# The first microseconds of a decoder layer: x and the first weight unit loaded in quarters by turns, the transposes of x spread around the first products

## The reference

```
x = x + 0.5 * swiglu(rms_norm(x, norm_ffn1), ffn1_gate, ffn1_up, ffn1_down)
h = rms_norm(x, norm_mix)
proj = h @ w_in                          # MoBA q k v | RWKV r k v | gate_A gate_B
y_a = moba_attention(qa, ka, va, rel_bias)
y_b = rwkv7_time_mix(h, rb, kb, vb, ...)
x = x + (sigmoid(ga) * (y_a @ proj_a) + sigmoid(gb) * (y_b @ proj_b)) @ w_out
x = x + 0.5 * swiglu(rms_norm(x, norm_ffn2), ffn2_gate, ffn2_up, ffn2_down)
return rms_norm(x, norm_final)
```

## Time and profile before

| what | us |
|---|---|
| median of 3 runs | 637.8 (637.66 to 638.42) |
| the profiled execution's own time | 637.18 |
| span of its trace, first to last instruction | 635.4 |
| TensorE busy | 626.1 (99% of the span) |
| VectorE busy | 422.8 (67%) |
| ScalarE busy | 295.6 (47%) |
| GpSimd busy | 91.3 (14%) |
| read from memory | 103.48 MB |

### The profile page before, as it was taken

One profiled execution on the slowest core, in us unless ns is written; L12 is line 12 of the kernel. 1 busy time (PEld: TensorE's weight loads), 2 busy tenths in 40 slices (PEclk: granted clock), 3 DMA queues, 4 the chain that ended last, 5 costly groups with the idle time before them and its releaser, 6 DMA issues.

```text
span 635.4 us, 15491 instructions
## 1 busy us (share of the span) xinstructions
PE 626.1 (99%) x6736; PEld 611.8 (96%) x6736; DVE 422.8 (67%) x491; ACT 295.6 (47%) x343; POOL 91.3 (14%) x91
## 2 busy tenths in 40 slices
PE   9999999999999999999999999999999999999996
PEld 9999999999999999999988999999999999999996
DVE  5856887665556369958994437977766666665662
ACT  6643555443334264525655545645544444443341
POOL 0017700000114000020004533006000000000120
PEclk9999999999999999999999999999999999999998
DMA  9686666545555246693242232346555566546541
GB/s 310 202 257 198 182 195 198 189 158 201 168 184 184 81 134 199 199 195 124 83 134 69 70 102 79 130 165 195 177 173 185 192 198 197 184 157 206 173 141 66
DMA packets 100640, 105.38 MB, mean 166 GB/s; under 512 B 2228, under 2 KB 98716, under 8 KB 100596
## 3 DMA queue, kind: packets, MB, share of 16 engines
q1 hardware_dynamic: 99380, 101.46, 49.5%
q0 software_dynamic: 1056, 3.02, 2.2%
q10 hardware_dynamic: 160, 0.27, 0.1%
HBM read 103.48 MB, written 1.25 MB: 165 GB/s over the span
## 4 chain that ended last, share of the span: by engine, by line
PE 90%; DVE 5%; DMA 2%; ACT 2%; issue 0%; DVEq 0%; ACTq 0%
PE two L1448 26%; PE two L1449 24%; PE two L1450 24%; PE two L1444 12%; DMA w_raw<-in_ffn_up 2%; DVE w_lo L894 2%; DVE hlo_f L913 1%; ACT w_hi L526 1%; DVE w_lo L904 1%; PE two L1716 1%; PE two L1717 1%; PE two L1718 1%; PE two L1859 0%; ACT KK L782 0%; PE two L1646 0%
## 5 line engine op out<-in xcount | busy, mean ns | idle before, releaser
L526 ACT ACTIVATE w_hi<-w_raw 128x2048 fp32r<-128x2048 f32 (+1 forms) x87 | 164.2, 1888 | 254.9 <-PE two L1450 220.1
L894 DVE TENSOR_TENSOR w_lo<-w_raw,w_hi 128x2048 fp32r<-128x2048 f32 (+1 forms) x87 | 202.4, 2326 | 85.9 <-ACT w_hi L526 85.5
L1448 PE MATMUL two<-hlo_f,w_hi 128*128 128x256 f32 x640 | 178.7, 279 | 1.0 <-DVE w_lo L894 0.9
L1449 PE MATMUL two<-hhi_f,w_lo 128*128 128x256 f32 x640 | 179.2, 280 | 0.0
L1450 PE MATMUL two<-hhi_f,w_hi 128*128 128x256 f32 x640 | 178.9, 280 | 0.0
L1448 PEld LDWEIGHTS two<-hlo_f,w_hi 128*128 128x128 f32 x640 | 120.3, 188 | 2.4 <-DVE w_lo L894 2.4
L1450 PEld LDWEIGHTS two<-hhi_f,w_hi 128*128 128x128 f32 x640 | 120.3, 188 | 0.0
L1449 PEld LDWEIGHTS two<-hhi_f,w_lo 128*128 128x128 f32 x640 | 120.2, 188 | 0.0
L1448 PE MATMUL two<-hid_lo_t,w_hi 128*128 128x256 f32 x352 | 98.6, 280 | 0.0
L1449 PE MATMUL two<-hid_hi_t,w_lo 128*128 128x256 f32 x352 | 98.4, 280 | 0.0
L1450 PE MATMUL two<-hid_hi_t,w_hi 128*128 128x256 f32 x352 | 98.3, 279 | 0.0
(11 more groups left out here) (339 smaller groups left out, 987.3 us busy)
## 6 DMA issues: line engine op xcount, KB each, us to landing
w_raw<-in_ffn_up SPq DMA_DIRECT2D x21, 1024.0 KB, 5.3
w_raw<-in_ffn_gate SPq DMA_DIRECT2D x20, 1024.0 KB, 5.4
w_raw<-in_w_in SPq DMA_DIRECT2D x20, 1024.0 KB, 5.0
w_raw<-in_ffn_down SPq DMA_DIRECT2D x16, 896.0 KB, 4.6
w_raw<-in_ffn_down SPq DMA_DIRECT2D x8, 1024.0 KB, 4.9
w_raw<-in_w_out SPq DMA_DIRECT2D x4, 1024.0 KB, 4.9
w_raw<-in_proj_a SPq DMA_DIRECT2D x4, 512.0 KB, 3.4
w_raw<-in_proj_b SPq DMA_DIRECT2D x4, 512.0 KB, 4.2
```

What stands on the lines that cost most here:

```text
L526: nc.scalar.activation(whi[slot][:, 0:kts], raw[slot][:, 0:kts], ACT.Copy).then_inc(sg["hi_ready"], 1)
L894: nc.vector.tensor_tensor(wlo[slot][:, 0:kts], raw[slot][:, 0:kts], whi[slot][:, 0:kts].bitcast(F32), ALU.subtract).then_inc(sg["lo_ready" ...
L1448: mm(dst, whi[slot][:, k_, cols], xl, start=start, stop=False)
L1449: mm(dst, wlo[slot][:, k_, cols], xh, start=False, stop=False)
```

## The change

- x is loaded in four quarters of 256 features (`x_in0` to `x_in3`), in turn with the four quarters of unit 0. The first four of these eight transfers are issued at once; each later one waits for the landing of an earlier one. The halves of unit 1 and `raw2` then wait for `x_in2`, `x_in3` and `w0_in3`.
- TensorE warms six times instead of seven, transposes the gain row, then the first two quarters of x, warms twice, transposes the third quarter, warms once, and begins unit 0. The fourth quarter of x is transposed behind the first 12 products of unit 0 (`if n + pair == 0`).
- Semaphores are joined: the gain row counts on `first_in` (then 32), `x_T` counts the gain row's transpose first (so `h_hi` waits for j + 2), and ScalarE takes the vectors behind `bias_row`, which is set by the product of `rel` that follows the vectors' transpose.
- ScalarE rounds each quarter of unit 0 behind a semaphore of its own; the squares of x wait for two quarters.

```diff
--- before.py
+++ after.py
@@ -119,7 +119,7 @@
 
 
 SIGNALS = """
-x_in0 x_in1 w0_mid w0_in w1_in vec_in first_in const_in gain1_in gain1_T gain1_ready vecT x_T x_loaded vec_ready
+x_in0 x_in1 x_in2 x_in3 w0_in1 w0_in2 w0_in3 w1_in vec_in first_in const_in gain1_ready x_T x_loaded vec_ready
 hi_ready lo_ready multiplied
 first_hi first_lo first_norm sq_one sq_sum last_sq mean_sq rms_ready rstd_ready gained hhi_ready hlo_ready
 gate_taken up_taken silu_done hid_prod hid_hi hid_lo down_first x_ffn_even x_ffn_odd
@@ -335,21 +335,30 @@
 
             xs = A["x"][0].rearrange("(j p) d -> p j d", p=P)
             sp.dma_start(cst[:, 0:C_FIRST], consts[:, 0:C_FIRST]).then_inc(sg["first_in"], 16)
-            for half in range(2):
-                ds = slice(half * D // 2, (half + 1) * D // 2)
-                sp.dma_start(x_tok[:, :, ds], xs[:, :, ds]).then_inc(sg[f"x_in{half}"], 16)
+
+            def x_quarter(q):
+                ds = slice(q * D // 4, (q + 1) * D // 4)
+                sp.dma_start(x_tok[:, :, ds], xs[:, :, ds]).then_inc(sg[f"x_in{q}"], 16)
 
             for f, base, down in FFN:
                 if f == 0:
+                    x_quarter(0)
                     sp.dma_start(raw[0][:, 0:2], gate_w[0][:, 0:2, 0:W]).then_inc(w_landed[0], 16)
-                    sp.dma_start(raw[0][:, 2:4], gate_w[0][:, 2:4, 0:W]).then_inc(sg["w0_mid"], 16)
+                    x_quarter(1)
+                    sp.dma_start(raw[0][:, 2:4], gate_w[0][:, 2:4, 0:W]).then_inc(sg["w0_in1"], 16)
                     sp.wait_ge(sg["x_in0"], 16)
-                    sp.dma_start(raw[0][:, 4:KD], gate_w[0][:, 4:KD, 0:W]).then_inc(sg["w0_in"], 16)
+                    x_quarter(2)
+                    sp.wait_ge(w_landed[0], 16)
+                    sp.dma_start(raw[0][:, 4:6], gate_w[0][:, 4:6, 0:W]).then_inc(sg["w0_in2"], 16)
                     sp.wait_ge(sg["x_in1"], 16)
+                    x_quarter(3)
+                    sp.wait_ge(sg["w0_in1"], 16)
+                    sp.dma_start(raw[0][:, 6:KD], gate_w[0][:, 6:KD, 0:W]).then_inc(sg["w0_in3"], 16)
+                    sp.wait_ge(sg["x_in2"], 16)
                     sp.dma_start(raw[1][:, 0:4], up_w[0][:, 0:4, 0:W]).then_inc(sg["w1_in"], 16)
-
-                    sp.wait_ge(w_landed[0], 16)
+                    sp.wait_ge(sg["x_in3"], 16)
                     sp.dma_start(raw[1][:, 4:KD], up_w[0][:, 4:KD, 0:W]).then_inc(w_landed[1], 16)
+                    sp.wait_ge(sg["w0_in3"], 16)
                     sp.dma_start(raw2, gate_w[0][:, :, W:2 * W]).then_inc(w_landed[0], 16)
                     sp.dma_start(cst[:, C_FIRST:C_ALL], consts[:, C_FIRST:C_ALL]).then_inc(sg["const_in"], 16)
                     for name in list(VECS)[1:]:
@@ -530,8 +539,8 @@
 
             def first_hi(n, i):
 
-                if n == 0 and i < 3:
-                    act.wait_ge((w_landed[0], sg["w0_mid"], sg["w0_in"])[i], 16)
+                if n == 0:
+                    act.wait_ge((w_landed[0], sg["w0_in1"], sg["w0_in2"], sg["w0_in3"])[i], 16)
                 elif n == 1 and i % 2 == 0:
                     act.wait_ge(w_landed[1] if i else sg["w1_in"], 16)
                 ks_ = slice(2 * i, 2 * i + 2)
@@ -547,7 +556,7 @@
             def h_hi(q, j, dst):
 
                 if q == 0:
-                    act.wait_ge(sg["x_T"], j + 1)
+                    act.wait_ge(sg["x_T"], j + 2)
                 elif q == 1:
                     act.wait_ge(sg["x_ffn_even"], j + 2)
                     act.wait_ge(sg["x_ffn_odd"], j + 2)
@@ -594,7 +603,7 @@
 
                 body(0, nexts(0) if f else [lambda: None, nexts(0)[1]])
                 if f == 0:
-                    act.wait_ge(sg["vecT"], 1)
+                    act.wait_ge(sg["bias_row"], 1)
                     nc.scalar.activation(vec[:, KD:NVEC], bank[5][:, KD:NVEC], ACT.Copy).then_inc(sg["vec_ready"], 1)
                 if f == 0:
                     for i in range(1, 8):
@@ -616,7 +625,7 @@
                     if s % 3 == 2 and s < NDOWN - 1 and f == 0:
                         h_hi(1, s // 3, hhi_m)
 
-            vector_rows(act, "norm_ffn1", sg["gain1_in"])
+            vector_rows(act, "norm_ffn1", sg["first_in"])
             act.wait_ge(sg["x_ffn_odd"], 1)
             nc.scalar.activation(idle[:, 0:1], idle[:, 0:1], ACT.Sqrt)
             act.wait_ge(sg["gain1_ready"], 1)
@@ -624,7 +633,8 @@
                 h_hi(0, j, hhi_f)
                 first_hi(0, j)
             for j in range(4):
-                act.wait_ge(sg[f"x_in{j // 2}"], 16)
+                for q in (0, 1) if j < 2 else (2, 3):
+                    act.wait_ge(sg[f"x_in{q}"], 16)
                 nc.scalar.activation(h_f[:, 2 * j:2 * j + 2].rearrange("p m t -> p (m t)"),
                                      x_tok[:, j % 2, j // 2 * (D // 2):(j // 2 + 1) * (D // 2)], ACT.Square,
                                      accum_out=tok[:, j:j + 1]).then_inc(sg["first_norm"], 1)
@@ -1031,7 +1041,7 @@
             nc.vector.memset(silu[:, 0, 0:P], 1.0).then_inc(sg["x_ffn_even"], 1)
             nc.vector.memset(idle[:], 0.0).then_inc(sg["x_ffn_odd"], 1)
 
-            dve.wait_ge(sg["gain1_T"], 1)
+            dve.wait_ge(sg["x_T"], 1)
             nc.vector.tensor_copy(vec[:, 0:KD], bank[5][:, 0:KD]).then_inc(sg["gain1_ready"], 1)
             dve.wait_ge(sg["gain1_ready"], 1)
             for j in range(4):
@@ -1505,6 +1515,8 @@
                             part(dst, whi[s][:, c, cols], hlo_f[:, c], m + c == 0)
                             part(dst, wlo[s][:, c, cols], hhi_f[:, c])
                             last = part(dst, whi[s][:, c, cols], hhi_f[:, c])
+                    if n + pair == 0:
+                        x_transposed(3)
                 last.then_inc(sg["multiplied"], 1)
 
             def ffn(f, base, down, q):
@@ -1522,7 +1534,7 @@
                     first_chunk(2)
                     pe.wait_ge(sg["vec_in"], 16 * len(VECS))
                     pe.wait_ge(sg["gain1_ready"], 1)
-                    nc.tensor.transpose(bank[5][:, 0:NVEC], vec_rows[:], ident[0:NVEC, 0:NVEC]).then_inc(sg["vecT"], 1)
+                    nc.tensor.transpose(bank[5][:, 0:NVEC], vec_rows[:], ident[0:NVEC, 0:NVEC])
                     pe.wait_ge(sg["const_in"], 16)
                     pe.wait_ge(sg["x_loaded"], 4)
                     mm(bank[6][0:H, 0:384], rel[:], cst[0:NB, C_HOT:C_HOT + 384], start=True, stop=True)\
@@ -1563,19 +1575,23 @@
                     part(bank[4][:, 0:P], silu[:, 0, 0:P], silu[:, 0, 0:P], True)
 
             pe.wait_ge(sg["x_ffn_even"], 1)
-            warm(7)
-            pe.wait_ge(sg["first_in"], 16)
-            pe.wait_ge(sg["gain1_in"], 16)
-            nc.tensor.transpose(bank[5][:, 0:KD], vec_rows[0:KD], ident[0:KD, 0:KD]).then_inc(sg["gain1_T"], 1)
-            warm(1)
-            for q in range(4):
-                pe.wait_ge(sg[f"x_in{q // 2}"], 16)
+            warm(6)
+            pe.wait_ge(sg["first_in"], 32)
+            nc.tensor.transpose(bank[5][:, 0:KD], vec_rows[0:KD], ident[0:KD, 0:KD]).then_inc(sg["x_T"], 1)
+
+            def x_transposed(q):
+                pe.wait_ge(sg[f"x_in{q}"], 16)
                 for c in range(2):
                     for j in range(2):
                         last = nc.tensor.transpose(bank[X_BANKS[q]][:, c * T + j * P:c * T + (j + 1) * P],
                                                    x_tok[:, j, (2 * q + c) * P:(2 * q + c + 1) * P], ident)
                 last.then_inc(sg["x_T"], 1)
-            warm(5)
+
+            x_transposed(0)
+            x_transposed(1)
+            warm(2)
+            x_transposed(2)
+            warm(1)
             ffn(0, N_FFN1, N_DOWN1, 0)
```

## The result

The changed kernel takes 639.32 us (median of 20 runs, 637.3 to 641.73), the kernel before 637.81 (20 runs, 635.75 to 641.9). The ratio is 1.0027, 95% interval 1.0018 to 1.0037: slower by 1.7 us, with 1.2 and 2.4 as ends. Forecast were no measurable change and 637.6, with 639.2 as the upper end.

The account below looks back on a forecast made before the run. TensorE, busy 99%, was taken as the bound, with early loads and splits setting its product at 39.31. Profiled 637.18 less 0.25 gave 636.93, on the median 637.55, said as 637.6; 8 in 10 from 636.7 to 639.2.

Parts of the forecast that it names:

- The landings: First transfers of x and unit 0: x0 lands at 4.21, each later quarter 0.78 us after, w3 at 9.7.
- The load of unit 3: Weight load on the chain, issued at 17.71 before: foreseen 0.25 us earlier, at 17.46, with its 5.52 us unchanged.
- the sum: Whole kernel: 637.18 less 0.25 for the shifted load gives 636.93; on the median 637.55, said as 637.6.
- Rival 2: First transfers: the queue runs thin with two or three quarters in flight, +0.1 to +0.4 us, 638.0; chance 0.20.
- the table: Foreseen landings at the start: x0 4.21, w0 4.99, x1 5.77, w1 6.55, x2 7.33, w2 8.1, x3 8.9, w3 9.7.
- Rival 1: Start of TensorE: first products reached at half pace, +1.3 us (+0.5 to +2.4), 639.1; chance 0.20.
- The front: First transposes and rounding: x0's transposes at 4.25, ScalarE's `hhi` at 5.41 instead of 6.31, 0.9 us early.
- pair 1 eats the gain: Unit 0 on TensorE: x3's transposes take 0.44 us before pair 1, leaving 0.4 of the 0.8 gained.
- SyncE's own queue: Issuing of transfers: SyncE free at about 16.7, 0.8 us of cover before the load of unit 3 at 17.46.
- The rest at nothing: Other parts of the change, such as SyncE's later issues and the vectors' later transpose: hidden, costing nothing.
- The range: Whole kernel's time: 636.7 to 639.2 us for 8 in 10; 637.1 to 638.0 for the forecast alone.

Follow-up runs that it names:

- g_half: Kernel before with the first quarter of unit 0 issued between the two halves of x; ratio 1.0034 (1.0018 to 1.0050).
- after: First trace of the changed kernel itself; 638.06 us in the profiled execution, 639.32 us as median of its runs.
- after2: The changed kernel once more, unaltered, for a second trace of its start; 637.65 us in that trace.
- a_nowait: Changed kernel without SyncE's waits between the first ten transfers, raw2 issued behind w0's landing; ratio to the kernel before 1.0033 (1.0018 to 1.0048).
- b_loads: Changed kernel's loads and waits alone, with TensorE's order of the kernel before; ratio to the kernel before 1.0055 (1.0034 to 1.0076).
- f_deep: Changed kernel without the three waits ahead of unit 1's halves and raw2; ratio to the kernel before 1.0012 (1.0001 to 1.0022).
- h_warm: Changed kernel with three warms ahead of x1's transposes and four behind, instead of none and two; ratio to the kernel before 1.0028 (1.0015 to 1.0042).
- k_deepwarm: Changed kernel without the waits ahead of unit 1's halves and raw2, plus more warms in TensorE's holes; ratio to the kernel before 1.0014 (1.0001 to 1.0027).
- i_x4r2: Kernel before with x in four transfers of 256 KB in 2 KB rows, timed and traced a second time; ratio 1.0011 (0.9999 to 1.0024).
- m_gdeep: Kernel before with a quarter of unit 0 between x's halves and no SyncE wait for x's second half ahead of unit 1; ratio 1.0053 (1.0040 to 1.0066).
- g_half2: Kernel before with a quarter of unit 0 between the halves of x, once more for a second trace; 638.79 us in that trace.
- c_pe: Changed kernel's TensorE order alone, with the loads and waits of the kernel before; ratio to the kernel before 1.0010 (0.9995 to 1.0025).

## Why the prediction was wrong

- **The landings** failed, and with them the forecast. "The size of a transfer thus does not matter while others are queued, and a quarter costs 0.78" was taken from halves and quarters that came one kind after the other. By turns it does not hold: x2 landed at 8.1 and 8.2 against 7.33, x3 at 10.2 and 10.5 against 8.9, w3 at 11.5 and 11.2 against 9.7. The loads alone cost 0.55%, one quarter of weights between two halves 0.34%, both with what the late x then does to TensorE.
- **The load of unit 3** was the other term: the sum let it move "if both loads take as long as before". In the first trace it was issued at 18.65, 1.2 behind the 17.46 of the forecast, and took 6.98 for the 5.52 of the earlier trace rows; so of the 2.4 that unit 3 is late, 0.9 lie before the issue and 1.5 in the load. In the second trace it was issued at 19.90 and took 5.54.
- **Rival 2** was the right mechanism for the part behind 8 us, and its sign (SyncE's waits over 0.3 later than the table) was there in both traces. It was given +0.1 to +0.4. Taking the three later waits away gave back more than half of the 1.7 (1.0027 to 1.0012) and again half (1.0028 to 1.0014), about 0.9 us each time. What was missed in it is that a late queue also lengthens the load that the chain crosses, and that "`raw2` is needed by ScalarE only after unit 1" had only as much cover as the 350 GB/s gave it.
- **Rival 1** happened in one trace of two of the changed kernel, in another form: the pace had doubled by 6.6, and then the granted clock fell to 0.50 at 8.5. Unit 3 was as late in that trace as in the first (2.5 and 2.4 us), but a mean clock of 0.995 or less is in only 2 of the 20 timed runs, and mending it gave nothing that the runs can tell. "If its pace doubles at 7.0 again" rested on one trace: in the second of the kernel before, the weight loads stood at full pace from 4.75 on. The rule of the Trainium skill ("TensorE: Matmul & The Clock Gate", Part 4: PE-mode transpose), by which the full clock does not engage for transposes because they do not count as busy in the same way, does not fit as it stands: in the first trace of the changed kernel the second four transposes began 0.12 apart (6.75 to the warm at 7.24) where the first four had stood 0.22 apart. As twelve warm instructions, the first transposes and a hole of 1.5 us stood ahead of them, what weight transposes have is not settled.
- **The front** was right: x0 at 4.03 (4.21 foreseen), `hhi` at 5.35 (5.41). So was it that pair 1 eats the gain. The first product came at 8.74 for 8.1 by the landing of x2, and bank 3 at 10.96 for 10.2 because its transposes stand behind the twelve products that began with it.
- **SyncE's own queue** did nearly what was feared: free at 18.5 instead of 16.7, with the load of unit 3 due at 18.63. It cost nothing, by 0.1.
- **The rest at nothing**, the joined semaphores and the later vector copy, shows in no chain.
- **The range** was built on the bounds of one trace's steady rates. Its upper end missed by 0.12; the spread of landings between executions, a microsecond at 5 us, was not in it.

Shown is that the loads cost and that about half of the loss is the three later waits. For the other half (1.0012 and 1.0014 with those waits away) no run names the cause. What also stays open is why turns of x and weights land late although all is issued. The trace gives the sixteen DMA engines' mean only; in g_half 1.5 MB had been moved by 7.0 us and x, which ends at 1.44 MB of the queue, landed at 8.6. That fits engines that are not equally far, but it was not measured.

## What to carry to other kernels

Cutting a first transfer so that work can begin sooner helps only the work that needs its first piece; ask when the last piece lands, and what is queued behind it. A chain of issues that each wait for a landing is priced by its last link, and by the load some 10 us later that finds the queue still full. When a start gets new holes, look at the granted clock and at the distance of the starts before putting a late product down to the transfers alone. Before trusting a microsecond of a start read from one trace, take a second trace, and let timed runs decide.

## What the runs showed of the hardware

- With quarters of x and of weights by turns the queues moved 204, 212, 281, 166, 260, 329 and 245 GB/s at 4 to 5 us in seven traces (after, after2, a_nowait, b_loads, f_deep, h_warm, k_deepwarm), with half a megabyte or more issued and not yet moved, against 367 and 352 in two of the kernel before.
- The same two transfers at the head of the same queue landed at 4.99, 4.85 and 6.0 in three executions.
- The granted clock fell from 1.00 to 0.50 in five traces, behind holes in TensorE's work: at 7.7 (i_x4r2; holes of 0.93 and 0.53 us), 8.5 (after2; 1.31 and 0.56), 8.6 (g_half; 2.41), 9.0 (m_gdeep; 1.96) and 9.7 (b_loads; 0.49, 0.74 and then idle from 8.8). With a hole of 1.50 and one of 0.25 it did not fall (after), nor with one of 0.99 (g_half2).
- Half pace also stands in the rows at a granted clock of 1.00: before the pace doubles for the first time, matmuls start at double distance. It doubled at 4.75 and 7.0 in two executions of the kernel before, at 10.0 in c_pe (a hole of 1.8 us at 4.2 to 6.0) and at 13.5 in a_nowait (holes of 0.6, 0.3 and 1.0 us). There the distance of the starts tells the pace, and the granted clock does not.
